# The last tile of the down projection by column halves, with two of five row blocks normed and stored during the second half

## The reference, cut

```python
def _rms_norm(x, g, eps=NORM_EPS):
    xf = x.astype(jnp.float32)
    y = xf * lax.rsqrt(jnp.mean(xf * xf, axis=-1, keepdims=True) + eps)
    return (y * g.astype(jnp.float32)).astype(x.dtype)

def _swiglu(h, w_gate, w_up, w_down):
    return (jax.nn.silu(h @ w_gate) * (h @ w_up)) @ w_down

    xp = xp + _swiglu(_rms_norm(xp, norm_ffn_g[l]), w_gate[l], w_up[l], w_down[l])
    xs = xs + _swiglu(_rms_norm(xs, norm_ffn_g[l]), w_gate[l], w_up[l], w_down[l])
y_prompt = _rms_norm(xp, norm_final_g)
y_sample = _rms_norm(xs, norm_final_g)
```

## Time and profile before

| | us |
|---|---|
| median of three runs | 1113.58 |
| lowest and highest | 1113.48, 1120.64 |
| the profiled execution, its own time | 1113.92 |
| its span | 1112.1 |
| outside of the span in that execution | 1.82 |
| granted TensorE clock, mean of the span | 0.941 |

### The profile page before, as it was taken

How to read it: one execution, slowest core, us unless ns; L and a number is a source line. 1 busy time by engine, 2 the same in 40 slices (tenths; PEclk the granted TensorE clock), 3 DMA queues, 4 the chain that set the end, 5 groups by cost and what they waited for, 6 DMA issues and landing times.

```text
span 1112.1 us, 29337 instructions
## 1 busy us (share of the span) xinstructions
PE 969.6 (87%) x11050; PEld 858.7 (77%) x11050; DVE 668.9 (60%) x1627; ACT 505.7 (45%) x1116; POOL 133.9 (12%) x69
## 2 busy tenths in 40 slices
PE   3989898998887779887889667899999999999995
PEld 3978787777764557676667554699999999999994
DVE  5389645675458887754346445788888888700003
ACT  5654543374125656645234262455555555611123
POOL 1322111111000010002111000000000000133330
PEclk8999999999988999888899787899999999999997
DMA  8699999999999999888979798386768686974632
GB/s 249 248 314 346 320 328 344 358 340 334 317 340 338 337 365 329 301 273 293 327 245 298 221 255 223 123 302 264 301 263 301 263 301 252 325 248 159 228 128 85
DMA packets 174933, 310.98 MB, mean 280 GB/s; under 512 B 13601, under 2 KB 87714, under 8 KB 173282
## 3 DMA queue, kind: packets, MB, share of 16 engines
q1 hardware_dynamic: 172898, 305.24, 80.3%
q10 hardware_dynamic: 1920, 4.20, 1.4%
HBM read 302.30 MB, written 73.92 MB: 338 GB/s over the span
## 4 chain that ended last, share of the span: by engine, by line
PE 32%; issue 30%; DMA 11%; SPq 11%; DVE 7%; ACT 7%; ACTq 0%; POOL 0%; DVEq 0%; POOLq 0%
PE ps L1383 11%; DMA v_ring<-in_cache_v_diff 6%; SPq L666 5%; PE ps L1038 5%; PE ps L1270 4%; PE ps L1232 4%; SPq L768 4%; DVE kt_sb L2153 2%; ACT q_st L1678 2%; PE ps L1189 2%; DMA k_ring<-in_state_v_win 2%; DMA k_ring<-in_cache_k_diff 2%; PE ps L1115 1%; DMA v_ring<-in_state_v_win 1%; ACT s_sb L1723 1%
## 5 line engine op out<-in xcount | busy, mean ns | idle before, releaser
L2153 DVE STREAM_TRANSPOSE kt_sb<-k_ring 128x512 f32<-128x512 f32 x336 | 220.5, 691 | 86.5 <-DMA k_ring<-in_cache_k_diff 37.4
L1270 PE MATMUL ps<-v_ring,pt_sb 128*32 128x128 f32 (+1 forms) x2496 | 98.8, 306 | 62.1 <-DMA v_ring<-in_cache_v_diff 49.3
L1270 PEld LDWEIGHTS ps<-v_ring,pt_sb 128*32 128x32 f32 (+1 forms) x2496 | 75.7, 121 | 78.1 <-issue 67.8
L1038 PE MATMUL ps<-h_hi,w_hi 128*128 128x288 f32 x384 | 124.4, 324 | 1.9 <-DVE h_lo L2006 1.9
L1038 PE MATMUL ps<-h_lo,w_hi 128*128 128x288 f32 x384 | 115.0, 299 | 0.0
L1038 PE MATMUL ps<-h_hi,w_lo 128*128 128x288 f32 x384 | 114.7, 299 | 0.0
L1232 PE MATMUL ps<-kt_sb,q_st 128*32 128x128 f32 (+1 forms) x2816 | 97.0, 281 | 10.2 <-DVE q_st L2163 4.6
L989 POOL TENSOR_TENSOR c_lo<-c_raw,c_hi 128x1408 fp32r<-128x1408 f32 x14 | 46.6, 3332 | 440.2 <-ACT c_hi L1781 440.2
L1232 PEld LDWEIGHTS ps<-kt_sb,q_st 128*32 128x32 f32 x2816 | 72.9, 114 | 28.2 <-issue 19.9
L1038 PEld LDWEIGHTS ps<-h_hi,w_hi 128*128 128x128 f32 x384 | 74.0, 193 | 16.1 <-issue 13.8
L949 POOL TENSOR_TENSOR w_lo<-w_raw,w_hi 128x1024 fp32r<-128x1024 f32 x24 | 57.3, 2390 | 229.5 <-ACT w_hi L1492 229.5
(11 more groups left out here) (236 smaller groups left out, 2289.4 us busy)
## 6 DMA issues: line engine op xcount, KB each, us to landing
k_ring<-in_cache_k_diff SPq DMA_DIRECT2D x256, 256.0 KB, 5.5
v_ring<-in_cache_v_diff SPq DMA_DIRECT2D x256, 256.0 KB, 5.5
out_k_win_sample<-in_state_k_win SPq DMA_DIRECT2D x32, 1020.0 KB, 8.3
out_v_win_sample<-in_state_v_win SPq DMA_DIRECT2D x32, 1020.0 KB, 8.5
k_ring<-in_state_k_win SPq DMA_DIRECT2D x32, 512.0 KB, 7.7
w_raw<-in_w_in SPq DMA_DIRECT2D x24, 512.0 KB, 6.3
g_raw<-in_w_gate SPq DMA_DIRECT2D x11, 1024.0 KB, 5.2
g_raw<-in_w_up SPq DMA_DIRECT2D x11, 1024.0 KB, 5.2
```

What stands on the lines that cost most here:

```text
L1038: last = nc.tensor.matmul(M[c][:, 0:HALF], wt, act[:, k, c * HALF:(c + 1) * HALF], start=k == 0 and at_first, stop=k == KT - 1 and act is ...
L1270: last = nc.tensor.matmul(O[32 * f:32 * f + 32, P * h:P * h + P], pt_sb[0:rows, 4 * f + b, :], values[:, f * P:(f + 1) * P], start=g == 0 ...
L2153: V.transpose(kt_sb[:, i, :], k_ring[:, i, :]).then_inc(kt_done, 1)
```

## The change

The two chunks of the last tile (46 and 47) are done for half 0 first, then for half 1. `product` gets an argument `halves`, `tok_transposes` the blocks. The order on PE is now: chunk 46 half 0, the five transposes of tile 6, chunk 47 half 0, chunk 46 half 1, the transposes of blocks 0 and 1 of tile 7, chunk 47 half 1, the transposes of blocks 2, 3 and 4. ACT copies each half by itself (`copy_half`). The residual add, the gain, the squares of the last 128 columns, mean, root, reciprocal and scale are done for blocks 0 and 1 first, and then for blocks 2 to 4. `product` counts `w_used` up once per call, so it reaches 50 at the end. SP's text is the same: it still waits for each block in turn.

```diff
-            def product(n, j, kts, bank, start=True, stop=True, k0=0, split_now=False):
+            def product(n, j, kts, bank, start=True, stop=True, k0=0, split_now=False, halves=range(2)):
...
-                        for c in range(2):
+                        for c in halves:
...
-            def tok_transposes(src, m_done):
-
-                for blk in range(NBLK):
+            def tok_transposes(src, m_done, blks=range(NBLK)):
+
+                for blk in blks:
...
             pe.wait_ge(e_copied, 2 * KT - 2)
-            product(C_ALL - 2, 0, DOWN_K, 1, stop=False)
+            product(C_ALL - 2, 0, DOWN_K, 1, stop=False, halves=(0,))
             turn_back(2 * KT - 2, 0)
-            product(C_ALL - 1, 1, DOWN_K, 1, start=False, k0=DOWN_K)
-            turn_back(2 * KT - 1, 1)
+            product(C_ALL - 1, 1, DOWN_K, 1, start=False, k0=DOWN_K, halves=(0,))
+            product(C_ALL - 2, 0, DOWN_K, 1, stop=False, halves=(1,))
+            pe.wait_ge(e_copied, 2 * KT)
+            pe.wait_ge(e_added, 2 * KT - 1)
+            tok_transposes(y_feat[:, 1, :], e_t, range(2))
+            product(C_ALL - 1, 1, DOWN_K, 1, start=False, k0=DOWN_K, halves=(1,))
+            pe.wait_ge(e_copied, 2 * KT + 1)
+            pe.wait_ge(e_added, 2 * KT)
+            tok_transposes(y_feat[:, 1, :], e_t, range(2, NBLK))
...
+            def copy_half(c):
+
+                act.wait_ge(w_used, C_ALL + 2 * c)
+                if c == 0:
+                    act.wait_ge(e_t, 2 * KT - 2)
+                nc.scalar.activation(y_feat[:, 1, HALF * c:HALF * (c + 1)], main_ps[:, 2 + c, 0:HALF], ACT.Copy)\
+                    .then_inc(e_copied, 1)
...
-            squares(slice(0, D - P), ss)
-            down_turn(7, 1, last=True)
+            squares(most, ss, range(0, 3), 2 * NBLK)
+            copy_half(0)
+            squares(most, ss, range(3, NBLK), 2 * NBLK + 3)
             act.wait_ge(e_added, 2 * KT)
-            squares(slice(D - P, D), rest)
-            act.wait_ge(meansq_done, 2 * NBLK + 2)
-            nc.scalar.activation(rms[:, 0:NBLK], ms[:, 0:NBLK], ACT.Sqrt).then_inc(rms_done, 1)
-            act.wait_ge(rstd_done, 2 * NBLK + 1)
-            act.wait_ge(xg_done, 2)
-            for blk in (1, 3):
-                nc.scalar.activation(xg_rows(blk), xg_rows(blk), ACT.Copy, scale=rstd[:, blk:blk + 1]).then_inc(y_scaled_act, 1)
+            squares(rest_cols, rest, range(0, 2), 3 * NBLK)
+            root_and_scale(0, 0, 2, 1)
+            copy_half(1)
+            act.wait_ge(e_added, 2 * KT + 1)
+            squares(rest_cols, rest, range(2, NBLK), 3 * NBLK + 2)
+            root_and_scale(1, 2, NBLK, 3)
...
+            def final_scale(part, c0, c1):
+
+                dve.wait_ge(sumsq_done, 3 * NBLK + c1)
+                V.tensor_tensor(ms[:, c0:c1], ss[:, 2 * NBLK + c0:2 * NBLK + c1], rest[:, c0:c1], ALU.add).then_inc(meansq_done, 1)
+                dve.wait_ge(meansq_done, 2 * NBLK + 2 * part + 1)
+                V.tensor_scalar(ms[:, c0:c1], ms[:, c0:c1], 1.0 / D, EPS, ALU.mult, ALU.add).then_inc(meansq_done, 1)
+                dve.wait_ge(rms_done, 2 * NBLK + part + 1)
+                V.reciprocal(rstd[:, c0:c1], rms[:, c0:c1]).then_inc(rstd_done, 1)
+                dve.wait_ge(rstd_done, 2 * NBLK + part + 1)
+                dve.wait_ge(xg_done, 2 + part)
+                for blk in range(c0, c1, 2):
...
             times_gain(slice(0, D - P))
-            residual(2 * KT - 1, KT - 1)
+            dve.wait_ge(e_t, 2 * KT)
+            V.tensor_tensor(x[:, 0:2, lasts], x[:, 0:2, lasts], tr_ps[:, 0, 0:2 * P].rearrange("p (b c) -> p b c", b=2), ALU.add)\
+                .then_inc(e_added, 1)
             dve.wait_ge(e_added, 2 * KT)
-            times_gain(slice(D - P, D))
+            times_gain(lasts, last=False)
+            final_scale(0, 0, 2)
+            dve.wait_ge(e_t, 2 * KT + 1)
+            V.tensor_tensor(x[:, 2:4, lasts], x[:, 2:4, lasts], tr_ps[:, 0, 2 * P:4 * P].rearrange("p (b c) -> p b c", b=2), ALU.add)
+            V.tensor_tensor(x[0:NS, 4:5, lasts], x[0:NS, 4:5, lasts], tr_ps[0:NS, 1:2, 0:P], ALU.add).then_inc(e_added, 1)
+            dve.wait_ge(e_added, 2 * KT + 1)
+            times_gain(lasts, b0=2)
+            final_scale(1, 2, NBLK)
```

More of the change, by code:

```diff
@@ L1938, in _, with squares @@
             down_turn(6, 0)
-            def squares(cols, sums):
-                for blk in range(NBLK):
+            def copy_half(c):
[4 more added lines that the diff above has]
+                    .then_inc(e_copied, 1)
+            def squares(cols, sums, blks, done):
+                for blk in blks:
                     r = ROWS[blk]
[L1944 to L1947, removed]
+                    act.wait_ge(sumsq_done, done + blk - blks[0])
                     at0 = 2 * NBLK if sums is ss else 0
@@ L1950, in squares, with root_and_scale @@
                                          accum_out=sums[0:r, at0 + blk:at0 + blk + 1]).then_inc(sumsq_done, 1)
+            def root_and_scale(part, c0, c1, blk):
+                act.wait_ge(meansq_done, 2 * NBLK + 2 * part + 2)
+                nc.scalar.activation(rms[:, c0:c1], ms[:, c0:c1], ACT.Sqrt).then_inc(rms_done, 1)
+                act.wait_ge(rstd_done, 2 * NBLK + part + 1)
+                act.wait_ge(xg_done, 2 + part)
+                nc.scalar.activation(xg_rows(blk), xg_rows(blk), ACT.Copy, scale=rstd[:, blk:blk + 1]).then_inc(y_scaled_act, 1)
             act.wait_ge(rstd_done, 2 * NBLK)
             nc.scalar.activation(row_max[0:1], rstd[0:1, 0:1], ACT.Sqrt)
+            most, rest_cols = slice(0, D - P), slice(D - P, D)
             act.wait_ge(e_added, 2 * KT - 1)
-            squares(slice(0, D - P), ss)
-            down_turn(7, 1, last=True)
+            squares(most, ss, range(0, 3), 2 * NBLK)
+            copy_half(0)
+            squares(most, ss, range(3, NBLK), 2 * NBLK + 3)
             act.wait_ge(e_added, 2 * KT)
-            squares(slice(D - P, D), rest)
-            act.wait_ge(meansq_done, 2 * NBLK + 2)
-            nc.scalar.activation(rms[:, 0:NBLK], ms[:, 0:NBLK], ACT.Sqrt).then_inc(rms_done, 1)
-            act.wait_ge(rstd_done, 2 * NBLK + 1)
-            act.wait_ge(xg_done, 2)
-            for blk in (1, 3):
-                nc.scalar.activation(xg_rows(blk), xg_rows(blk), ACT.Copy, scale=rstd[:, blk:blk + 1]).then_inc(y_scaled_act, 1)
+            squares(rest_cols, rest, range(0, 2), 3 * NBLK)
[4 more added lines that the diff above has]
+            root_and_scale(1, 2, NBLK, 3)
         @block.vector
@@ L2571, in _, with times_gain @@
                 residual(m + KT, m)
-            def times_gain(cols):
+            def times_gain(cols, b0=0, last=True):
                 n = cols.stop - cols.start
-                V.tensor_tensor(xg[:, 0:4, cols], x[:, 0:4, cols], g_final[:, cols].unsqueeze(1).to_broadcast([P, 4, n]), ALU.mult)
-                V.tensor_tensor(xg4[0:NS, cols], x[0:NS, 4, cols], g_final[0:NS, cols], ALU.mult).then_inc(xg_done, 1)
+                mul = V.tensor_tensor(xg[:, b0:4 if last else 2, cols], x[:, b0:4 if last else 2, cols],
+                                      g_final[:, cols].unsqueeze(1).to_broadcast([P, (4 if last else 2) - b0, n]), ALU.mult)
+                if last:
+                    mul = V.tensor_tensor(xg4[0:NS, cols], x[0:NS, 4, cols], g_final[0:NS, cols], ALU.mult)
+                mul.then_inc(xg_done, 1)
+            def final_scale(part, c0, c1):
[8 more added lines that the diff above has]
+                for blk in range(c0, c1, 2):
+                    r = ROWS[blk]
+                    V.tensor_scalar(xg_rows(blk)[0:r], xg_rows(blk)[0:r], rstd[0:r, blk:blk + 1], None, ALU.mult)\
+                        .then_inc(y_scaled, 1)
+            last_m = KT - 1
+            lasts = slice(last_m * P, D)
             dve.wait_ge(norm_in[2], 16)
```

11 lines of the change are left out of this document (removed).

## The result

The changed kernel took 1104.63 us (median of seven executions, 1100.49 to 1113.59) against 1113.48 for the kernel before on the same occasion (seven, 1109.73 to 1120.64): a ratio of 0.9927 with an interval of 0.9899 to 0.9955. The profiled execution took 1107.77 with a span of 1106.0.

What follows compares the result with a forecast made beforehand. The last stretch was taken as bound by output bytes, after PE and 5.48 us of small operations. Scale 1.38 earlier plus 2.61 of bytes gave 4.0 us off 1113.58, so 1109.6 us, range 1108.4 to 1111.5.

Steps and rivals of the forecast that it cites:

- PE: Last tile's matmuls, same number and size plus two inner transposes: last matmul 0.22 us later, nothing for one PSUM bank.
- The small operations: Between last matmul and scale: smaller copy, three transposes, smaller add and three squares take 1.60 us off 5.48.
- The output: Stores of blocks 0 and 1 leave early, under PE and small operations: 1.05 MB or 2.61 us less at the end.
- the unchanged landing: Lower bound for the output: last issue still takes 4.8 us to land, so only 2.1 us are won.
- the short landing: Upper bound for the output: sample rows land in 2.7 us, data staying in line, so about 3.2 us are won.
- The covers: Slack before moved work delays anyone: ACT 1.0 us before its second copy, POOL's low part 0.6, PE's inner transposes 3.9.
- The sum: Scale 1.38 us earlier plus 2.61 us of output bytes: 3.99 us off the end of the kernel.
- Within 1% of no change: Whole kernel: chance 0.97 that the time stays within 1%, about 11 us; the change is worth 0.36%.
- an execution-to-execution scatter of a few tenths: Whole kernel: the part of the forecast range allowed for time differences between executions, a few tenths of a us.
- Rival B: At the end, the last DMA's landing, not bytes ahead, sets the finish, or early stores issue too late; 1112.2 us, chance 0.08.
- Rival C: Last tile: matmuls running into one PSUM bank wait for it, costing 21 us, about 1131 us; chance 0.02.
- the rule on small operations: Tail operations on VectorE and ScalarE: the Trainium skill says fixed latency per instruction, paid per small tile, against splitting.

Runs made afterwards that it cites:

- r4: The kernel before with only the last tile's matmuls reordered by column halves on PE, one copy and norm at the end; median 1115.38 us, ratio 0.9999.
- r3: The changed kernel with outputs of blocks 0 and 1 issued only once block 2 is scaled; median 1112.79 us, ratio 0.9963; 31.0 us from last tile's start to end.
- r7: The changed kernel with block 2 scaled in two pieces and stored by two DMAs; 1108.84 us, ratio 0.996; 28.2 us from last tile's start to end.

## Why the prediction was right and wrong

Right, by its own steps:
- PE: 0.22 later; 0.24 measured. No price for one bank, by r4.
- The small operations: 1.60 less; 1.61. The copy took 0.42, three transposes 0.56, the add 0.42 and 0.20, a square 0.43 with its hand-over.
- The output: 2.61 less; 2.55, and r3 shows by itself that it is these bytes. Of the two bounds, the unchanged landing (2.1) and the short landing (3.2), neither held; the value of the bytes did. (The prediction shows no working for the 3.2, nor for the 1.65 from the scale to the last issue, which measured 1.63; the forecast uses neither.)
- The covers: ACT's wait 1.05 where 1.0 was foreseen, POOL's 0.6 as foreseen, no wait of PE at the inner transposes.
- The sum: 3.99; 3.92 from the last tile's start.
- The time: 1109.6 against a median of 1109.48 over 43 executions. That is luck: the median that the forecast starts from, 1113.58, is 0.7 below the 1114.29 of 112 executions, and the 43 contain the seven low ones, without which their median is 1110.44.
- Within 1% of no change: the ratio is 0.9927, and 0.9962, 0.9978 and 0.9947 on the other occasions. The timing is finer than the 1% that the prediction gave it; seven executions of each kernel gave 0.3% to either side.

Wrong: the range. The step that failed is the term of the range that the prediction put as "an execution-to-execution scatter of a few tenths". The scatter has a standard deviation of 3.8 us in the kernel before. It sat in the table shown, where the third of three times was 7 us above the other two; the forecast took the median of the three as if it were good to a few tenths. The measured median of seven lay 5.0 under the forecast. The range should have been worked out from that table. The prediction also judged how far the time could fall by the last 14 us alone, and left out that the first 700 us move. A median of seven at this deviation is uncertain by 1.25 x 3.8 / 2.65 = 1.8 (2.65 is the root of seven), the median of three that it starts from by 2.7, together 3.3, and for 8 times in 10 that is some 4.2 to either side, 1105.4 to 1113.8. Even that misses 1104.63 by 0.8, and whether chance alone took the first occasion there stays open, as said above. The terms of the sum were off by 0.1 at most; the scatter of a median of seven is eighteen times that.

Rival B was given 0.08 and named as its ground the 4.8 of the half-sized last DMA. (Its time, 1112.2, leaves out the "some tenths" that it names.) That landing was long because of the queue: with two stores fewer ahead it was 4.3. Rival C, at 0.02, was rightly kept small by the rows of another stage. The duration that the prediction sets beside the rule on small operations, 0.411 for 288 columns, is of a copy out of PSUM; for operands in SBUF the squares show the same form, 0.31 for 128 columns in the changed kernel and 0.95 for 896.

## What to carry to other kernels

When all outputs leave at the end, look in the windows whether the end is made of bytes at the full rate, as here. Each part that can be finished under the last matmuls was then worth its bytes over that rate, an estimated 1.3 us for 512 KB at 402 GB/s. Reordering the matmuls to get there cost nothing here, as the same run in one bank elsewhere in the trace had said, but look at the cover of the engine that must come back for the second half.
For a change of a few tenths of a per cent read the trace from a mark behind the part that scatters, and take the range from the spread of the given times, not from the terms.

## What the runs showed of the hardware

The same program took from 1105.32 to 1123.29 us in 112 executions. In its three traces all of the difference comes before the gate products; from the first gate product on, the traces of one program agree to 0.1 us over 400 (four traces of the changed kernel do so too). Taking the DMA share from 0.96 to 0.74 left the spread at 8 us over six executions.
An issue of a store on SP took 0.33 to 0.43 us with none or one of 512 KB just ahead of it (the changed kernel), 0.78 or 0.79 with two (the changed kernel), and up to 1.20 to 1.22 with three or four (r3). In r7, with smaller stores ahead (two of 256 KB, then one of 512), the fourth took 0.51.
The shortest landing of a 512 KB store was 2.6 us (2.7 in the kernel before). That of the 256 KB of sample rows was 4.8 behind four such stores, and 4.3 with only two of the four just ahead.
The outputs ran at 381 to 418 GB/s in the full microseconds with all 16 DMA engines busy, and at 221 to 262 in the last such one, though the engines were as busy (shares of 0.97 to 1.07; the earlier trace rows, the changed kernel, r3).
